# Retention of one decoder layer: score products within blocks of 128, preceding blocks through prefix sums of keys times values

## Chip, cores and metric

One core of a Trainium2 chip runs the kernel in one launch. The metric is device time in microseconds (us): the median over runs of the same program. TensorE is called PE here, VectorE DVE, ScalarE ACT, GpSimd POOL, and SyncE SP (it only issues transfers).

## The reference, cut to what matters

One layer for a prompt of 512 tokens and 8 sample tokens (D = 1024). The part that the change touches is the retention of the prompt, 4 heads of 128 columns, from a zero state:

```
q, k = rope(q), rope(k) * 128 ** -0.5
# for each head: gamma = 1 - 2 ** (-5 - head); for tokens r (query) and s (key)
o[r]  = sum over s <= r of gamma ** (r - s) * (q[r] . k[s]) * v[s]
s_new = sum over s of gamma ** (511 - s) * outer(k[s], v[s])       # an output
oc    = o - mean(o over its 128 columns)                            # then RMS norm, gain, silu gate
```

The reference itself walks over chunks of 128 tokens with a carried state; the sums are the same. Behind the mixer come the output projection, a router, 32 experts (top 2 of 8 in the best of 4 groups) and a gated per-layer embedding.

## The kernel before

PE works through a list of jobs written out in `job_list` (L52 to L75). Job number n writes the pair of PSUM banks n mod 4, so PE starts a job only when the engines that read job n - 4 are done with it (`Plan.free`, L138; READERS, L81, names the readers: A is ACT, D is DVE). All engines walk the same list in the same order: PE from L1613, ACT from L784, DVE from L1204. Each job ends with an increment of `pe_jobs`, and each reader counts up `act_jobs` or `dve_jobs`. The jobs around the change:

- **Chunks** ("q", "k", "v", "g", "gc", "hc", "gb", "wo"): a projection of 128 columns for all 520 tokens, 48 matmuls at L1563. Weights are split in two halves of fewer bits for each chunk: ACT makes the high half (L758), DVE the low half (`low_half`, L1147), both two chunks ahead. PE waits for both before a chunk.
- **q and k** are rotated after their chunk: ACT copies the swapped halves (L827, L828), then DVE runs three linked instructions (L1253 to L1255). PE needs the rotated rows for the scores.
- **scA, scB** (L1667): key block j (128 tokens) against queries of block j and all later ones, in widths 512, 384, 256 and 128, four matmuls for a head. DVE multiplies each by the decay while it reads PSUM (L1279 to L1284).
- **kt** (L1671): four transposes of the keys; DVE scales them (L1288), and then centres the values of the head over their 128 columns (`centre`, L1172: a reduction and a subtraction) into `v_mid`.
- **pv** (L1678): centred values times masked scores, again widths 512 to 128, accumulated in one bank, and copied by ACT (L838). With centred values the output needs no mean taken off later.
- **st** (L1684): four 128x128 products of scaled keys and values, accumulated into the state of the prompt; copied by ACT (L841), stored by POOL (L644).
- **gc, hc, gb**: the convolution. DVE's part of an hc job is long (L1309 to L1326).
- **state_row** (L1162): the state update of one of the 8 sample tokens, two DVE instructions 512 wide (L1167, L1169). VB_AT (L90) says after which chunks they run. All 8 must be done before PE starts "so" (L1654), the sample tokens' output. DVE centres that, "ot" transposes it (L1662), ACT squares the output of all four heads (L802), and "vs" (L1638) sums the squares. ACT takes the root, DVE the reciprocal (L1229), POOL stores it and loads it broadcast (L650, L653), and DVE waits for that in the first gate job, g0 (L1296).

In a head the order is scA, scB, kt, one chunk, pv, st, another chunk. After the projections (to about 260 us) come the router, an indirect load of the first expert's rows, and the experts, whose weights SP loads (2 MB a unit, three units an expert). The loads from unit 9 on wait for the experts' matmuls to free a slot (L551 to L568).

The original score and value products:

```
for half, j in enumerate((0, 1) if kind == "scA" else (2, 3)):
    width = SEQ - j * P
    last = mm(b[:, half * 512:half * 512 + width], kT[:, j * P:(j + 1) * P], qT[:, j * P:SEQ], ...)
```

Of the kernel before, what the change touches and what calls it, by code (L numbers as in the profile page):

```python
# [23 lines left out]
P = 128  # L24
# [9 lines left out]
H = 4  # L34
# [17 lines left out]
def job_list():  # L52

    jobs = [("v", 0), ("v", 1), ("v", 2), ("ss", 0), ("v", 3), ("rb", 0)]
    jobs += [("q", 0), ("vt", NT - 1), ("vt", 0), ("k", 0), ("vt", 1), ("vt", 2), ("q", 1), ("vt", 3)]

    def scores(h):
        return [("scA", h), ("scB", h), ("kt", h)]

    def sums(h):  # L60
        return [("pv", h), ("st", h)]
# [12 lines left out]
    jobs += [("rk", 0), ("ix", 0), ("iy", 0), ("tot", 0)]  # L74
    return jobs  # L75
# [4 lines left out]
LG_CUT = 256  # L80
READERS = dict(ss="A", rb="D", q="AD", k="AD", v="A", vt="A", g="D", so="D", ot="D", scA="D", scB="D", kt="D",  # L81
               pv="A", st="A", vs="A", lt="D", gc="D", hc="D", gb="D", wo="D", tp="A", lg="D",
               rk="D", ix="D", iy="D", tot="D", u="D", pa="A", pb="A", pg="A")
# [74 lines left out]
def build(nc, a, o):  # L158
# [9 lines left out]
    with ExitStack() as ctx:  # L168
# [86 lines left out]
        temp = ring[:, TEMP_SLOT, :]  # L255
        masked = [temp[:, i * 1280:(i + 1) * 1280] for i in range(2)]
        kd = [temp[:, 2560 + i * 512:3072 + i * 512] for i in range(2)]
        st_out = temp[:, 3584:4096].rearrange("p (h e) -> p h e", h=H)
        sq = [region_q[:, i * T:(i + 1) * T] for i in range(2)]
# [28 lines left out]
        o_few = sin_t[0:NB, 0:H * P]  # L288
        decay = region_d[:, :].rearrange("p (h r) -> p h r", h=H)
        gate_c = [region_z[:, i * T:(i + 1) * T] for i in range(2)]  # L290
# [86 lines left out]
        u_high, squared, sum_ready = sem("u_high"), sem("squared"), sem("sum_ready")  # L377
        silu_g, v_centred, o_squared, ret_made = sem("silu_g"), sem("v_centred"), sem("o_squared"), sem("ret_made")
        head_rstd, r_few_stored, r_wide_loaded = sem("head_rstd"), sem("r_few_stored"), sem("r_wide_loaded")
# [77 lines left out]
        def _(sp):  # L457
# [36 lines left out]
            for n in range(WIN_SLOTS, len(CHUNKS)):  # L494
# [6 lines left out]
                if n == 22:  # L501

                    sp.wait_ge(dve_jobs, HEAD.done("D", ("scB", H - 1)))
                    load_spare(0, 0)
                if n == 24:

                    sp.wait_ge(pe_jobs, HEAD.pe(("st", H - 1)))
                    sp.wait_ge(ret_stored, 16)
                    load_first(1)
# [107 lines left out]
        def _(pool):  # L617
# [24 lines left out]

            pool.wait_ge(act_jobs, HEAD.done("A", ("st", H - 1)))
            pool.dma_start(o["ret_p"], st_out).then_inc(ret_stored, 16)  # L644
# [93 lines left out]
        def _(act):  # L738
# [45 lines left out]
            for n, (kind, c) in enumerate(JOBS):  # L784
# [226 lines left out]
        def _(dve):  # L1011
# [192 lines left out]
            for n, (kind, c) in enumerate(JOBS):  # L1204
# [63 lines left out]
                elif kind == "ot":  # L1268
                    V.tensor_copy(qk[:, 0:H, SEQ:T], b[:, 0:H * NB].rearrange("p (h n) -> p h n", h=H)).then_inc(
                        dve_jobs, 1)  # L1270
                elif kind in ("scA", "scB"):

                    if (kind, c) == ("scA", 0):
# [3 lines left out]
                    dst = masked[c % 2]  # L1277
                    if kind == "scA":
                        link(V.tensor_tensor(dst[:, 0:512], b[:, 0:512], decay[:, c, 0:512], ALU.mult))  # L1279
                        V.tensor_tensor(dst[:, 512:896], b[:, 512:896], decay[:, c, 0:384],  # L1280
                                        ALU.mult).then_inc(dve_jobs, 1)
                    else:
                        link(V.tensor_tensor(dst[:, 896:1152], b[:, 0:256], decay[:, c, 0:256], ALU.mult))
                        V.tensor_tensor(dst[:, 1152:1280], b[:, 512:640], decay[:, c, 0:128],  # L1284
                                        ALU.mult).then_inc(dve_jobs, 1)
                elif kind == "kt":

                    V.tensor_tensor(kd[c % 2].rearrange("p (t d) -> p t d", t=4),  # L1288
                                    b[:, 0:512].rearrange("p (t d) -> p t d", t=4),
# [246 lines left out]
        def _(pe):  # L1536
# [76 lines left out]
            for n, (kind, c) in enumerate(JOBS):  # L1613
# [45 lines left out]
                elif kind == "ot":  # L1659
                    after("D", ("so", 0))  # L1660
                    for h in range(H):
                        last = tr(b[:, h * NB:(h + 1) * NB], o_few[:, h * P:(h + 1) * P], ident[0:NB, 0:NB])  # L1662
                elif kind in ("scA", "scB"):
                    kT, qT = qk[:, H + c, :], qk[:, c, :]
                    for half, j in enumerate((0, 1) if kind == "scA" else (2, 3)):
                        width = SEQ - j * P
                        last = mm(b[:, half * 512:half * 512 + width], kT[:, j * P:(j + 1) * P], qT[:, j * P:SEQ],  # L1667
                                  start=True, stop=True)
                elif kind == "kt":
                    for j in range(4):  # L1670
                        last = tr(b[:, j * P:(j + 1) * P], qk[:, H + c, j * P:(j + 1) * P], ident[:, :])  # L1671
                elif kind == "pv":
                    after("D", ("scB", c))
                    pe.wait_ge(v_centred, c + 1)
                    at = 0
                    for j in range(4):
                        width = SEQ - j * P
                        last = mm(b[:, j * P:SEQ], v_mid[:, j, c * P:(c + 1) * P], masked[c % 2][:, at:at + width],  # L1678
                                  start=(j == 0), stop=(j == 3))
                        at += width  # L1680
                elif kind == "st":
                    after("D", ("kt", c))
                    for j in range(4):
                        last = mm(b[:, 0:P], kd[c % 2][:, j * P:(j + 1) * P], v_rows[:, j, c * P:(c + 1) * P],  # L1684
                                  start=(j == 0), stop=(j == 3))
                elif kind == "tp":
# [208 lines left out]
def small_constants():  # L1895
# [8 lines left out]
    sin = np.sin(ang).astype(np.float32)  # L1904
    diff = np.arange(SEQ)[None, :] - np.arange(P)[:, None]
    decay = np.stack([np.where(diff >= 0, np.exp(np.float64(g) * np.maximum(diff, 0)), 0.0) for g in lg], 1) * SCALE
    left = (SEQ - 1 - np.arange(SEQ)).reshape(4, P).T
    kdec = np.stack([np.exp(np.float64(g) * left) for g in lg], 1) * SCALE
    token = np.zeros((P, NT), np.float32)
    for t, (r0, m) in enumerate(TILES):  # L1910
# [11 lines left out]
        cos=np.concatenate([cos, cos]), sin=np.concatenate([-sin, sin]),  # L1922
        decay=decay.reshape(P, H * SEQ).astype(np.float32), ident=np.eye(P, dtype=np.float32),
        meanw=np.full((P, P), 1.0 / P, np.float32),
# [78 lines left out]
```

## Time and profile before

| what | us |
|---|---|
| median of 3 runs | 830.74 (829.55 to 832.31) |
| profiled execution, its own time | 831.13 |
| its span in the trace | 829.3 |
| PE busy / DVE busy / ACT busy | 727.8 / 283.5 / 180.7 |

The trace is one execution; its time differs from the median by 0.39 us, and 1.8 us of it lie outside the span. Matmuls are pipelined in the records, so a single one's duration (272 ns and more) is longer than its share of a stream; the chain of waits gives the time from start to start. A float32 matmul shows as two records.

### The profile page before, as it was taken

To read this page: it belongs to the slowest core of one execution; us is meant where nothing else is said; L and a number is where in the kernel's file an instruction comes from. 1 tells how busy PE (TensorE), PEld (TensorE's weight loads), DVE (VectorE), ACT (ScalarE), POOL (GpSimd) and SP (SyncE) were. 2 spreads that over 40 slices of the span, in tenths; PEclk is the share of its full clock that TensorE was granted. 3 is DMA by queue.
4 is the path that set the end of the run, shared out by engine and by line. 5 is a ranking of instruction groups with operands and counts; after the bars stand their busy time and mean duration, and the time that the engine had idled before them with its cause. 6 is when DMAs were issued, how large, how long until landed. Compare 5 with 4: busy or idle time off the path is not lost.

```text
span 829.3 us, 11240 instructions
## 1 busy us (share of the span) xinstructions
PE 727.8 (88%) x4496; PEld 449.1 (54%) x4496; DVE 283.5 (34%) x504; ACT 180.7 (22%) x278; POOL 102.8 (12%) x161
## 2 busy tenths in 40 slices
PE   8999999999999789899999887777777777778996
PEld 8988899999998534333333322222222222226775
DVE  5556579766434521111101001001001001005875
ACT  7242321323322100111111110000000000004576
POOL 0500000000001112121121111111111111100000
PEclk9999999999999899999999999999999999999999
DMA  9641126572945799999999999999999999995301
GB/s 347 234 180 52 61 80 228 203 261 77 394 155 192 229 393 417 424 427 424 426 427 422 428 425 427 425 427 428 425 428 427 426 427 426 426 422 208 131 27 77
DMA packets 36457, 258.39 MB, mean 312 GB/s; under 512 B 7905, under 2 KB 8465, under 8 KB 22841
## 3 DMA queue, kind: packets, MB, share of 16 engines
q1 hardware_dynamic: 27248, 237.17, 70.0%
q0 software_dynamic: 7072, 19.07, 6.1%
q10 hardware_dynamic: 2096, 1.56, 0.6%
q8 instruction: 31, 0.51, 0.3%
q14 instruction: 10, 0.07, 0.0%
HBM read 251.04 MB, written 15.14 MB: 321 GB/s over the span
## 4 chain that ended last, share of the span: by engine, by line
PE 50%; DMA 35%; DVE 5%; ACT 2%; issue 2%; SPq 0%; DVEq 0%; POOLq 0%; ACTq 0%
DMA arena<-in_w_exp 33%; PE ps L1563 20%; PE ps L1759 15%; PE ps L1776 5%; PE ps L1890 2%; PE ps L1606 1%; PE ps L1678 1%; DMA region_u<-h_rows,index 1%; PE ps L1667 1%; DVE xh L1426 1%; DVE region_u L1379 1%; PE ps L1571 1%; DMA region_m<-y_rows 1%; PE ps L1767 1%; DMA y_rows<-region_v,both_cols 1%
## 5 line engine op out<-in xcount | busy, mean ns | idle before, releaser
L1759 PE MATMUL ps<-arena,region_u 128*64 128x512 f32 x960 | 218.9, 602 | 47.0 <-DMA arena<-in_w_exp 46.0
L1759 PEld LDWEIGHTS ps<-arena,region_u 128*64 128x64 f32 x960 | 67.0, 138 | 196.8 <-issue 124.7
L1375 DVE SCALAR_TENSOR_TENSOR region_u<-ps,small,region_u 128x256 f32<-128x256 f32 x32 | 15.5, 483 | 377.2 <-ACT region_u L864 377.2
L1563 PE MATMUL ps<-u_hi,w_hi 128*128 128x260 f32 x448 | 128.3, 286 | 4.5 <-issue 2.3
L1563 PE MATMUL ps<-u_lo,w_hi 128*128 128x260 f32 x448 | 126.6, 283 | 0.0
L1563 PE MATMUL ps<-u_hi,w_low 128*128 128x260 f32 x448 | 126.5, 282 | 0.0
L1776 PE MATMUL ps<-arena,region_u 128*64 128x512 f32 x480 | 109.6, 598 | 5.9 <-DVE region_u L1379 2.5
L1563 PEld LDWEIGHTS ps<-u_hi,w_hi 128*128 128x128 f32 x448 | 84.3, 188 | 6.2 <-issue 4.2
L1563 PEld LDWEIGHTS ps<-u_hi,w_low 128*128 128x128 f32 x448 | 84.5, 189 | 0.0
L1563 PEld LDWEIGHTS ps<-u_lo,w_hi 128*128 128x128 f32 x448 | 84.4, 188 | 0.0
L685 POOL DMA_INDIRECT y_rows<-region_v,both_cols x32 | 33.4, 1042 | 368.1 <-ACT region_v L868 368.1
L864 ACT ACTIVATE region_u<-ps,small 128x256 f32<-128x256 f32 x32 | 15.1, 473 | 267.3 <-PE ps L1759 267.3
L1776 PEld LDWEIGHTS ps<-arena,region_u 128*64 128x64 f32 x480 | 33.2, 136 | 63.0 <-issue 54.4
L868 ACT ACTIVATE region_v<-ps 128x512 f32<-128x512 f32 x32 | 19.1, 597 | 158.7 <-PE ps L1776 158.7
L1147 DVE TENSOR_TENSOR w_low<-arena,w_hi 128x1024 fp32r<-128x1024 f32 x35 | 42.6, 1220 | 20.2 <-ACT w_hi L758 20.0
L758 ACT ACTIVATE w_hi<-arena 128x1024 fp32r<-128x1024 f32 x35 | 36.7, 1049 | 25.0 <-PE ps L1563 24.9
L1563 PE MATMUL ps<-mix_lo,w_hi 128*128 128x260 f32 x128 | 36.2, 283 | 0.0
L1767 PE MATMUL ps<-ident,region_u 128*128 128x128 f32 x64 | 13.5, 293 | 25.4 <-DVE region_u L1375 25.3
L679 POOL DMA_INDIRECT region_u<-h_rows,both_cols x30 | 31.3, 1043 | 25.7 <-POOL both_cols L700 25.7
L1767 PEld LDWEIGHTS ps<-ident,region_u 128*128 128x128 f32 x64 | 7.1, 140 | 50.3 <-DVE region_u L1375 48.0
L1890 PE MATMUL ps<-gate_hi,u_hi 128*128 128x512 f32 (+1 forms) x72 | 26.8, 373 | 1.3 <-DVE u_lo L1449 1.3
L1890 PE MATMUL ps<-gate_lo,u_hi 128*128 128x512 f32 (+1 forms) x72 | 26.5, 367 | 0.0
(284 smaller groups left out, 855.8 us busy)
## 6 DMA issues: line engine op xcount, KB each, us to landing
arena<-in_w_exp SPq DMA_DIRECT2D x88, 2048.0 KB, 26.9
arena<-in_w_in SPq DMA_DIRECT2D x35, 512.0 KB, 4.3
region_q<-in_w_exp SPq DMA_DIRECT2D x24, 256.0 KB, 10.3
arena<-in_w_exp SPq DMA_DIRECT2D x8, 512.0 KB, 4.1
arena<-in_w_ple_gate SPq DMA_DIRECT2D x2, 2048.0 KB, 23.5
region_u<-in_xt SPq DMA_DIRECT2D x2, 1040.0 KB, 6.1
arena<-in_state_ret POOLq DMA_DIRECT2D x2, 1024.0 KB, 8.9
xh<-v_few POOLq DMA_DIRECT2D x1, 2048.0 KB, 9.1
```

The source lines that it names most:

```text
L679: pool.indirect_dma_start(out=xg[b], out_offset=None, in_=h_rows, in_offset=bass.IndirectOffsetOnAxis(ap=at, axis=0), bounds_check=2 * T - ...
L685: pool.indirect_dma_start(out=y_half, out_offset=bass.IndirectOffsetOnAxis(ap=scol[:, b:b + 1], axis=0), in_=out_sb[b], in_offset=None, bo ...
L758: nc.scalar.activation(w_hi[n % WIN_HIGH], w_raw[:, n % WIN_SLOTS, :], ACT.Copy).then_inc(w_hi_ready, 1)
L864: nc.scalar.activation(sg[b], ps[:, 2 + b, 0:256], ACT.Silu, scale=rs[b]).then_inc(out_sem, 1)
L868: nc.scalar.activation(out_sb[b], ps[:, 6 + b, :], ACT.Copy).then_inc(out_sem, 1)
L1147: V.tensor_tensor(w_low[:, n % WIN_SLOTS, :], w_raw[:, n % WIN_SLOTS, :], w_hi[n % WIN_HIGH], ALU.subtract).then_inc(w_lo_ready, 1)
L1375: V.scalar_tensor_tensor(hs[b], ps[:, 2 + b, 256:512], rs[b], sg[b], ALU.mult, ALU.mult).then_inc(out_sem, 1)
L1563: last = mm(halves(out)[:, half, :], w[:, k, :], u[:, cols], start=(k == 0 and s == 0), stop=(k == KD - 1 and s == 2))
L1759: last = mm(ps[side * 64:side * 64 + 64, 2 + b, :], xv[:, k // 4, k % 4, :], rows(k % 4 * 2 + side), start=(k == 0), stop=(k == KD - 1))
L1767: last = tr(ps[:, 4 + b, k * P:(k + 1) * P], hs[b][:, k * P:(k + 1) * P], ident[:, :])
L1776: last = mm(ps[side * 64:side * 64 + 64, 6 + b, :], hv, rows(q * 2 + side), start=(q == 0), stop=(q == 3))
L1890: last = mm(b[:, cols], u[:, k, :], w, start=(k == 0 and i == 0), stop=(k == KD - 1 and i == 2))
```

## The change

The scores are taken within a block only: four matmuls of width 128 for a head in one job, "sc". What earlier blocks give comes through the products that "st" already makes: they are no longer accumulated on PE but left as four separate sums. DVE forms the prefix sums, the last of which is the state output, then centres the three that are needed (`s_mid`), and PE multiplies them with `q_far`, the queries of tokens 128 to 511 times gamma ** (r - 511). The decay table keeps its size and holds both factors. `masked` and `kd` have one buffer instead of two. The order of jobs is new: in a head sc, kt, chunk, st, chunk, pv. gb0 moves up into the fourth head. Seven of the state updates run later by a chunk or two, and so, ot and vs stand after gc2, hc2 and gb2 instead of after hc1, gb1 and gc2.

```diff
-    jobs += scores(0) + [("k", 1)] + sums(0) + [("q", 2)] + scores(1) + [("k", 2)] + sums(1) + [("q", 3)]
-    jobs += scores(2) + [("k", 3)] + sums(2) + [("gc", 0)] + scores(3) + [("hc", 0)] + sums(3)
-    conv = [(kind, c) for c in range(CC) for kind in ("gc", "hc", "gb")]
-    between = [("so", 0), ("ot", 0), ("vs", 0)]
-    for n, job in enumerate(conv[2:]):
-        jobs += [job] + (between[n - 2:n - 1] if n >= 2 else [])
+    head = [("k", 1), ("q", 2), ("k", 2), ("q", 3), ("k", 3), ("gc", 0), ("hc", 0), ("gb", 0)]
+    for h in range(H):
+        jobs += [("sc", h), ("kt", h), head[2 * h], ("st", h), head[2 * h + 1], ("pv", h)]
+    between = {("gc", 2): ("so", 0), ("hc", 2): ("ot", 0), ("gb", 2): ("vs", 0)}
+    for job in [(kind, c) for c in range(1, CC) for kind in ("gc", "hc", "gb")]:
+        jobs += [job] + ([between[job]] if job in between else [])
...
-VB_AT = {("gc", 0): (0, 1), ("hc", 0): (2,), ("gb", 0): (3, 4, 5), ("gc", 1): (6, 7)}
+VB_AT = {("gc", 0): (0,), ("gb", 0): (1, 2, 3), ("gc", 1): (4, 5), ("gb", 1): (6, 7)}
...
-                elif kind == "st":
-
-                    nc.scalar.activation(st_out[:, c, :], b[:, 0:P], ACT.Copy).then_inc(act_jobs, 1)
...
-                    if kind == "scA":
-                        link(V.tensor_tensor(dst[:, 0:512], b[:, 0:512], decay[:, c, 0:512], ALU.mult))
-                        V.tensor_tensor(dst[:, 512:896], b[:, 512:896], decay[:, c, 0:384],
-                                        ALU.mult).then_inc(dve_jobs, 1)
-                    else:
-                        link(V.tensor_tensor(dst[:, 896:1152], b[:, 0:256], decay[:, c, 0:256], ALU.mult))
-                        V.tensor_tensor(dst[:, 1152:1280], b[:, 512:640], decay[:, c, 0:128],
-                                        ALU.mult).then_inc(dve_jobs, 1)
+                    link(V.tensor_tensor(q_far, qk[:, c, P:SEQ], far[:, c, :], ALU.mult))
+                    V.tensor_tensor(masked.rearrange("p (j r) -> p j r", j=4), b[:, 0:SEQ].rearrange("p (j r) -> p j r", j=4),
+                                    decay[:, c, :].unsqueeze(1).to_broadcast([P, 4, P]), ALU.mult).then_inc(dve_jobs, 1)
+                elif kind == "st":
+
+                    sums = b[:, 0:SEQ].rearrange("p (j e) -> p j e", j=4)
+                    link(V.tensor_copy(s_mid[:, 0, :], sums[:, 0, :]))
+                    for j in (1, 2):
+                        link(V.tensor_tensor(s_mid[:, j, :], s_mid[:, j - 1, :], sums[:, j, :], ALU.add))
+                    V.tensor_tensor(st_out[:, c, :], s_mid[:, 2, :], sums[:, 3, :], ALU.add).then_inc(dve_jobs, 1)
+                    dve.wait_ge(dve_jobs, done)
+                    centre(s_mid, s_mid, col["vm"][:, 0:3], [P, 3, P]).then_inc(s_centred, 1)
...
-                elif kind in ("scA", "scB"):
-                    kT, qT = qk[:, H + c, :], qk[:, c, :]
-                    for half, j in enumerate((0, 1) if kind == "scA" else (2, 3)):
-                        width = SEQ - j * P
-                        last = mm(b[:, half * 512:half * 512 + width], kT[:, j * P:(j + 1) * P], qT[:, j * P:SEQ],
-                                  start=True, stop=True)
+                elif kind == "sc":
+                    for j in range(4):
+                        at = slice(j * P, (j + 1) * P)
+                        last = mm(b[:, at], qk[:, H + c, at], qk[:, c, at], start=True, stop=True)
...
-                    at = 0
+                    pe.wait_ge(s_centred, c + 1)
                     for j in range(4):
-                        width = SEQ - j * P
-                        last = mm(b[:, j * P:SEQ], v_mid[:, j, c * P:(c + 1) * P], masked[c % 2][:, at:at + width],
-                                  start=(j == 0), stop=(j == 3))
-                        at += width
+                        at = slice(j * P, (j + 1) * P)
+                        last = mm(b[:, at], v_mid[:, j, c * P:(c + 1) * P], masked[:, at], start=True, stop=(j == 0))
+                        if j:
+                            last = mm(b[:, at], s_mid[:, j - 1, :], q_far[:, (j - 1) * P:j * P], start=False, stop=True)
...
                     for j in range(4):
-                        last = mm(b[:, 0:P], kd[c % 2][:, j * P:(j + 1) * P], v_rows[:, j, c * P:(c + 1) * P],
-                                  start=(j == 0), stop=(j == 3))
+                        at = slice(j * P, (j + 1) * P)
+                        last = mm(b[:, at], kd[:, at], v_rows[:, j, c * P:(c + 1) * P], start=True, stop=True)
```

## Rows read from the trace of the kernel before

**Rows 1.** The page's chain that ended last: shares of the span by engine.

```profile
PE 50%; DMA 35%; DVE 5%; ACT 2%; issue 2%; SPq 0%; DVEq 0%; POOLq 0%; ACTq 0%
```

**Rows 2.** Stretches: length, busy time of PE, PEld, DVE, ACT, POOL, PEclk, DMA share, GB/s.

```profile
218.00:262.00 44.00, 43.72 (x392) 41.69 (x391) 14.86 (x22) 12.43 (x24) 3.88 (x6) 1.00 0.53 186
285.00:296.00 11.00, 9.79 (x36) 3.15 (x37) 4.22 (x16) 0.47 (x1) 1.40 (x3) 0.79 0.92 318
310.00:436.00 126.00, 120.91 (x582) 44.71 (x578) 17.40 (x44) 13.22 (x24) 25.18 (x40) 1.00 1.01 425
436.00:748.00 312.00, 243.24 (x1112) 81.62 (x1108) 33.19 (x80) 25.02 (x48) 46.91 (x76) 1.00 1.01 426
```

**Rows 3.** Chain that ended last, one head of retention: start us, us, what.

```profile
58.36 0.63 PE ps L1671 x4
58.99 5.77 PE ps L1563 x48
...
66.91 0.89 PE ps L1684 x8
67.81 5.73 PE ps L1563 x48
73.54 2.16 PE ps L1667 x8
75.69 0.44 PE ps L1671 x4
...
77.27 5.99 PE ps L1563 x48
83.26 2.16 PE ps L1678 x8
```

**Rows 4.** DVE's instructions in order of time, 60 to 77 us.

```profile
60.64 0.29 DVE L1284 TENSOR_TENSOR arena<-ps,region_d 128x128 f32<-128x128 f32 x1
61.04 0.69 DVE L1288 TENSOR_TENSOR arena<-ps,small 128x512 f32<-128x512 f32 x1
62.96 1.22 DVE L1147 TENSOR_TENSOR w_low<-arena,w_hi 128x1024 fp32r<-128x1024 f32 x1
...
75.00 0.70 DVE L1253 TENSOR_TENSOR region_q<-ps,trig 128x520 f32<-128x520 f32 x1 [4.67 <-ACT region_z L828]
...
76.47 0.70 DVE L1255 TENSOR_TENSOR region_q<-region_q,region_z 128x520 f32<-128x520 f32 x1
```

**Rows 5.** Chain that ended last, behind the heads and at the experts' start.

```profile
121.94 17.20 PE ps L1563 x144
...
146.94 0.34 PE ps L1662 x4
147.28 5.94 PE ps L1563 x48
...
275.84 7.03 DMA region_u<-h_rows,index
...
285.03 9.41 PE ps L1759 x32
...
300.20 6.89 PE ps L1759 x32
```

**Rows 6.** DVE in order of time: an hc job, first and last; the reciprocal.

```profile
139.21 0.06 DVE L1309 MEMSET region_z<- 128x2 f32 x1 [0.66 <-PE ps L1563]
...
143.40 0.69 DVE L1326 TENSOR_TENSOR region_m<-arena 128x512 f32<-128x512 f32 x1
...
155.04 3.40 DVE L1229 RECIPROCAL region_q<-region_q 128x520 f32<-128x520 f32 x1 [0.85 <-ACT region_q L843]
```

**Rows 7.** ACT in order of time: the squares between ot and vs.

```profile
149.17 2.20 ACT L802 ACTIVATE region_q<-region_q 128x520 f32<-128x520 f32 x4
```

**Rows 8.** DMA issues: the broadcast that g0 waits for, KB, us to landing.

```profile
region_q<-r_few POOLq DMA_DIRECT2D x1, 1040.0 KB, 7.7
```

**Rows 9.** PE's waits by line and releaser: us in total, times, longest.

```profile
PE ps L1759 <- DMA arena<-in_w_exp: 46.0, 39, 1.4
```

**Rows 10.** Weight loads of the 128-wide products st: min, median, max ns.

```profile
L1684 PEld LDWEIGHTS ps<-region_v,arena x32: 192/192/192, 66.6 to 121.6; 128*128 128x128 f32 x32
```

More of the change, by code:

```diff
@@ L80 @@
 LG_CUT = 256
-READERS = dict(ss="A", rb="D", q="AD", k="AD", v="A", vt="A", g="D", so="D", ot="D", scA="D", scB="D", kt="D",
-               pv="A", st="A", vs="A", lt="D", gc="D", hc="D", gb="D", wo="D", tp="A", lg="D",
+READERS = dict(ss="A", rb="D", q="AD", k="AD", v="A", vt="A", g="D", so="D", ot="D", sc="D", kt="D",
+               pv="A", st="D", vs="A", lt="D", gc="D", hc="D", gb="D", wo="D", tp="A", lg="D",
                rk="D", ix="D", iy="D", tot="D", u="D", pa="A", pb="A", pg="A")
@@ L255, in build @@
         temp = ring[:, TEMP_SLOT, :]
-        masked = [temp[:, i * 1280:(i + 1) * 1280] for i in range(2)]
-        kd = [temp[:, 2560 + i * 512:3072 + i * 512] for i in range(2)]
-        st_out = temp[:, 3584:4096].rearrange("p (h e) -> p h e", h=H)
+        masked, kd = temp[:, 0:SEQ], temp[:, SEQ:2 * SEQ]
+        st_out = temp[:, 2 * SEQ:3 * SEQ].rearrange("p (h e) -> p h e", h=H)
+        q_far = temp[:, 3 * SEQ:4 * SEQ - P]
+        s_mid = temp[:, 4 * SEQ - P:5 * SEQ - 2 * P].rearrange("p (j e) -> p j e", j=3)
         sq = [region_q[:, i * T:(i + 1) * T] for i in range(2)]
@@ L288, in build @@
         o_few = sin_t[0:NB, 0:H * P]
-        decay = region_d[:, :].rearrange("p (h r) -> p h r", h=H)
+        decay = region_d[:, 0:H * P].rearrange("p (h r) -> p h r", h=H)
+        far = region_d[:, H * P:H * SEQ].rearrange("p (h r) -> p h r", h=H)
         gate_c = [region_z[:, i * T:(i + 1) * T] for i in range(2)]
@@ L377, in build @@
         u_high, squared, sum_ready = sem("u_high"), sem("squared"), sem("sum_ready")
-        silu_g, v_centred, o_squared, ret_made = sem("silu_g"), sem("v_centred"), sem("o_squared"), sem("ret_made")
+        silu_g, v_centred, s_centred, o_squared, ret_made = (
+            sem("silu_g"), sem("v_centred"), sem("s_centred"), sem("o_squared"), sem("ret_made"))
         head_rstd, r_few_stored, r_wide_loaded = sem("head_rstd"), sem("r_few_stored"), sem("r_wide_loaded")
@@ L501, in _ @@
                 if n == 22:
-                    sp.wait_ge(dve_jobs, HEAD.done("D", ("scB", H - 1)))
+                    sp.wait_ge(dve_jobs, HEAD.done("D", ("sc", H - 1)))
                     load_spare(0, 0)
                 if n == 24:
-                    sp.wait_ge(pe_jobs, HEAD.pe(("st", H - 1)))
+                    sp.wait_ge(pe_jobs, HEAD.pe(("pv", H - 1)))
                     sp.wait_ge(ret_stored, 16)
@@ L641, in _ @@
             pool.dma_start(o["conv_s0"], a["state_conv"][:, 1, :]).then_inc(misc_stored, 16)
-            pool.wait_ge(act_jobs, HEAD.done("A", ("st", H - 1)))
+            pool.wait_ge(dve_jobs, HEAD.done("D", ("st", H - 1)))
             pool.dma_start(o["ret_p"], st_out).then_inc(ret_stored, 16)
@@ L1662, in _ @@
                         last = tr(b[:, h * NB:(h + 1) * NB], o_few[:, h * P:(h + 1) * P], ident[0:NB, 0:NB])
[L1663 to L1668 removed]
+                elif kind == "sc":
+                    for j in range(4):
+                        at = slice(j * P, (j + 1) * P)
+                        last = mm(b[:, at], qk[:, H + c, at], qk[:, c, at], start=True, stop=True)
                 elif kind == "kt":
@@ L1672, in _ @@
                 elif kind == "pv":
-                    after("D", ("scB", c))
+                    after("D", ("sc", c))
                     pe.wait_ge(v_centred, c + 1)
-                    at = 0
+                    pe.wait_ge(s_centred, c + 1)
                     for j in range(4):
-                        width = SEQ - j * P
-                        last = mm(b[:, j * P:SEQ], v_mid[:, j, c * P:(c + 1) * P], masked[c % 2][:, at:at + width],
-                                  start=(j == 0), stop=(j == 3))
-                        at += width
+                        at = slice(j * P, (j + 1) * P)
+                        last = mm(b[:, at], v_mid[:, j, c * P:(c + 1) * P], masked[:, at], start=True, stop=(j == 0))
+                        if j:
+                            last = mm(b[:, at], s_mid[:, j - 1, :], q_far[:, (j - 1) * P:j * P], start=False, stop=True)
                 elif kind == "st":
@@ L1904, in small_constants @@
     sin = np.sin(ang).astype(np.float32)
-    diff = np.arange(SEQ)[None, :] - np.arange(P)[:, None]
+    diff = np.arange(P)[None, :] - np.arange(P)[:, None]
     decay = np.stack([np.where(diff >= 0, np.exp(np.float64(g) * np.maximum(diff, 0)), 0.0) for g in lg], 1) * SCALE
+    far = np.stack([np.tile(np.exp(np.float64(g) * (np.arange(P, SEQ) - SEQ + 1)), (P, 1)) for g in lg], 1)
+    decay = np.concatenate([decay.reshape(P, H * P), far.reshape(P, H * (SEQ - P))], 1)
     left = (SEQ - 1 - np.arange(SEQ)).reshape(4, P).T
@@ L1922, in small_constants @@
         cos=np.concatenate([cos, cos]), sin=np.concatenate([-sin, sin]),
-        decay=decay.reshape(P, H * SEQ).astype(np.float32), ident=np.eye(P, dtype=np.float32),
+        decay=decay.astype(np.float32), ident=np.eye(P, dtype=np.float32),
         meanw=np.full((P, P), 1.0 / P, np.float32),
```

9 lines of the change are left out of this document (2 added, 7 removed).

## The prediction, made before the changed kernel ran

> **What bounds the kernel now.** I read the shares of the chain first: half of the span is PE, a third is DMA [rows 1]. The stretches tell where. Up to the output projection PE is busy all the time, with its clock at the full 2.4 GHz level [rows 2]. From about 290 us on the DMA engines are full: share 1.01 from 310 to 748 us, at 425 GB/s, while PE has slack behind 436 us. So the experts are bound by the weight stream. Its length is fixed by its bytes, and its start by PE: the loads of unit 9 and later wait until the first expert's matmuls free a slot. Between 218 and 262 us the DMA share is 0.53, so no old traffic holds that start back. So whatever the retention stage saves on PE moves the first expert, the stream and the end by as much. The stages behind are unchanged, and the change is worth what it is worth in PE's chain between 54 and 154 us.
>
> In that chain [rows 3] PE is the bound but for one thing: the next key chunk starts only when the query chunk before it is rotated. The query chunk ends at 73.54, DVE's last rotation instruction ends at 76.47 + 0.70 = 77.17 [rows 4], and the key chunk starts at 77.27, 3.73 us behind the query chunk's end. PE fills 2.60 of these with scores and transposes and idles 1.14. The chunk behind the idle time then takes 5.99 us instead of 5.74.
>
> **PE's work.** Scores: 1280 columns for a head take 2.16 us (L1667, eight records), or 0.108 us for 128 columns of a record. What is new is 128 columns wide throughout, and the nearest row of such products is st: eight records in 0.89 us, 0.111 each. I take 0.111. Scores: 8 x 0.111 = 0.89, so 1.27 less for each head. pv: four products within blocks and three with the prefix sums, 14 records, 1.55 us instead of 2.16, 0.60 less. st has the same products (their start flags cost nothing: the count of columns is the same) and kt is untouched. Over four heads that is 7.5 us less work; how much of it reaches the end depends on what PE waits for.
>
> **Start to start on PE.**
> - Head 0. kt0 waits today for the rotation of q1 and starts at 58.36; k1 follows at 58.99. In the new order kt0 reuses an older bank pair and runs earlier, but k1 waits for the same rotation, so it starts at 58.36: 0.63 gained. It then carries the 0.22 that follow an idle spell (5.99 against 5.77). Gain 0.41. PE's idle time there grows to about 2.0 us.
> - From the end of k1 to the start of k2. Today: pv 2.16 + st 0.89 + q2 5.73 + 3.73 = 12.51. New: st 0.89 + q2 5.73 + 3.73 = 10.35. pv (1.55), sc (0.89) and kt (0.44) are 2.88 and lie within the 3.73, which the rotation sets; 0.85 stay idle. Gain 2.16: here the order hides the whole of pv. From k2 to k3 the same. Together 4.3.
> - From the end of k3 to the end of pv3: pv2, scores 3 and pv3 are shorter by 0.60 + 1.27 + 0.60 = 2.47.
>
> Sum 7.2 us, if no new wait comes.
>
> **DVE's work, and the waits that it adds.** Per head DVE loses the multiplications of widths 512, 384, 256 and 128 and gains q_far (384) and one of 512, about 0.75 less. It gains the sums: a copy and three additions 128 wide, 0.29 each with 0.03 between them [rows 4], then a reduction and a subtraction 384 wide. For 384 I take 0.56, between 0.29 for 128 and 0.69 for 512. With 0.1 where it waits for its own result or for PE: 1.3 + 1.2 + 0.2 = 2.7 us. The bounds are 2.2 (every instruction at 0.29) and 4.5 (every one at 0.69). ACT loses its copy of st, 4 times, which nobody waits for.
>
> PE needs the centred sums at pv. With K the end of a key chunk: rotation ends at K + 3.63, the sums at K + 6.3; PE has done st and the chunk behind it at K + 0.89 + 5.74 = K + 6.63. So pv0, pv1 and pv2 have 0.3 us to spare. Behind the sums DVE has the low half of a chunk (1.22) before the next rotation, which ACT's copies let start 1.46 behind the query chunk; that leaves 0.57.
>
> pv3 is different: between hc0 and st3 DVE works off hc0, from 0.07 behind PE's end to 4.26 later at the last instruction's start and 0.69 more [rows 6], so 4.95. The sums are there at 4.95 + 2.7 = 7.65 behind hc0's end, while PE has st3 and gb0 done at 0.89 + 5.74 = 6.63. **PE waits 1.0 us at pv3.** Behind that wait on PE stands gc1, and everything after it.
>
> State updates: each is two instructions 512 wide, 1.4. The second to fourth run behind gb0, the next two behind gc1, the last two behind gb1. With F the end of gb0, and the low halves (1.22), evacuations (0.70) and hc1 in between, I get the eighth done at F + 23.9, while PE, with pv3 behind it and four chunks, gets to so at F + 25.7. Cost nothing; without these 1.8 us of cover, so waits.
>
> **so, ot and vs one group later.** Here I see the second new wait. Today ot stands behind gb, on which DVE has just 0.70 us of work, so the squares are early. In the new list ot stands behind hc2, and DVE finishes the whole convolution first. With T the end of hc2: ot's copy is done at T + 5.3, ACT's four squares take 2.20 [rows 7], so T + 7.6, and PE can start vs at T + 7.7. PE has ot (0.34) and gb2 (5.94) behind it at T + 6.28 [rows 5]. **PE waits 1.4 us at vs.** The way to g0 gets shorter too: PE is at the end of g0 by about T + 32, four chunks behind vs. The squares, ACT's high half (about 1.0, as DVE's 1.22), DVE's low half and evacuation of gb2, ACT's copy of it, the root and the reciprocal of 3.40 end near T + 15.5; the broadcast lands in 7.7 [rows 8], and if the store before it took as long, the end would be T + 31. It is hidden, also past POOL's other transfers, which are done by then. SP's loads around it (units 0 and 1, behind chunk loads) wait for the same jobs and have tens of us before the experts.
>
> Each new wait also makes PE's next work some 0.2 longer (0.63 against 0.44 for kt, 5.99 against 5.74 for a chunk): 0.4 for both.
>
> **Sum.** 7.2 - 1.0 - 1.4 - 0.4 = 4.4, taken as 4.3 for the extra semaphore wait at each pv. Against the profiled execution 831.13 - 4.3 = 826.8; against the median, which is 0.39 lower, 830.74 - 4.3 = **826.4 us**.
>
> **Rivals.**
> - *The two waits do not come* (DVE ahead of my walk): 830.7 - 7.2 = 823.6. For it: the sums' lower bound of 2.2 takes half off pv3's wait. Against: ot behind hc2 is plain order on DVE. Chance 0.12, still faster.
> - *The clock.* PE idles 7 us before the first expert, and the stretch behind it ran at a granted clock of 0.79; its 32 matmuls took 9.41 instead of 6.89 [rows 2, 5]. PE's idle spells of up to 1.4 us left the clock at 1.00 [rows 9, 2]. The new 2.0 us at k1 lies between. If it costs the same 2.5 us: 828.9, within the noise. Chance 0.06. It can hardly happen twice, as the other waits are no longer than those that held.
> - *128 columns do not pay.* If the weight load showed behind every narrow product, 192 ns each [rows 10], scores would take 1.54 and pv 2.69. Then pv, sc and kt are 4.67, no longer within 3.73; k1 to k3 gain 1.2 each, the rest loses 0.44, and with both waits the gain is about 0.0: 830.7. Against: the st row itself, 0.89 for eight, shows loads hidden. Chance 0.03. The Trainium skill, page "TensorE: Matmul & The Clock Gate", section "Back-to-back issue gap", gives about 81 ns for a sustained pair of load and matmul of 128 columns against about 131 ns for 512. By that, as an estimate, narrower scores would shrink by about a third only, pv with its 14 records would get longer, and the change would bring next to nothing on PE. This trace disagrees: its time goes by columns, 0.108 against 0.111.
> - *Hidden by the stream or given back later*: no change, 830.7. Against: the load's start follows PE. Chance 0.05.
> - *Slower: DVE's sums become the bound, at every pv.* If the chain took x us more than 2.7, pv3 costs x, pv2 x - 0.3, the rotations of q2 and q3 x - 0.57 each, so the gain is 5.7 - 4x. It is slower by over 0.3% from x = 2.1, a chain of 4.8; at 5.0 it gives 834.2. For it: six dependent short instructions right in front of what PE waits for. Against: even with all at 0.69 it is 4.5, 832. Chance 0.05.
>
> **How the numbers follow.** About 0.3%, 2.5 us, is what a measurement of this kernel can tell from no change. My forecast has 0.69 and is faster; with the first rival 0.81, of which I give 0.02 to same for a pv wait longer than I have it. Same: 0.06 + 0.03 + 0.05 + 0.02, less a little that goes to either side: 0.15. Slower 0.05. Low end: the first rival less the spread of runs, 822.8. High end: clock rival and sums of 3.2 us, 829.3.
>
> **What would show it right or wrong.** In the chain of the changed kernel: scores in 0.89 and pv in 1.55 for a head; about 10.35 from the end of k1 to the start of k2, set by the rotation; PE idle 2.0 before k1, 0.85 before k2 and k3, 1.0 before pv3 on the centred sums and 1.4 before vs on ACT's squares; the first expert's matmuls near 285.0 - 4.3 = 280.7; the clock at 1.00 from 54 to 154 us. The sum is wrong if the sums on DVE take over 3 us, if pv0 to pv2 wait, or if the stream does not start earlier with the first expert.

## The result and the profile after

The changed kernel takes 825.31 us (median of 6 runs, 821.47 to 827.34), the kernel before on the same occasion 830.32 (828.78 to 832.31). The ratio is 0.994 (95% interval 0.9921 to 0.9959): faster by 5.0 us, where 4.3 were forecast. On two later occasions the same kernel took 822.49 and 822.29 beside 829.35 and 829.71, so the gain lies between 5 and 7.5 us, by the occasion. The profiled execution took 825.39, with a span of 823.6.

The chain that ended last, for heads 0 and 1 (start us, us, what). Line numbers have moved: L1647 is vt3 (the last transposes of the values, the landmark from which stages are measured below), L1560 a chunk, L1663 the scores, L1666 kt, L1680 st, L1673 and L1675 the seven products of pv (two records each).

```profile
54.54 0.44 PE ps L1647 x4
54.98 0.91 PE ps L1663 x8
55.88 0.69 ACT region_v L832
56.57 1.69 issue
58.27 7.53 PE ps L1560 x48
65.79 0.89 PE ps L1680 x8
66.68 5.74 PE ps L1560 x48
...
74.32 0.89 PE ps L1663 x8
75.21 0.44 PE ps L1666 x4
75.65 0.51 issue
76.16 6.01 PE ps L1560 x48
82.17 0.89 PE ps L1680 x8
83.06 5.74 PE ps L1560 x48
88.80 0.44 PE ps L1673 x4
...
90.36 0.89 PE ps L1663 x8
91.25 0.44 PE ps L1666 x4
91.69 0.84 issue
92.53 5.98 PE ps L1560 x48
```

The scores take 0.89 us instead of 2.16, pv 1.56 (88.80 to 90.36) instead of 2.16. From the end of k1 (65.79) to the start of k2 (76.16) are 10.37 us, and 10.36 from k2 to k3; the kernel before has 12.51 [rows 3]. One thing is off: k1, behind the longer idle time, takes 7.53 us instead of the 5.77 of [rows 3].

The same profile in stretches (us; length; busy time of PE, PEld, DVE, ACT, POOL; PEclk, DMA share, GB/s): the clock fell to half (1.2 GHz) when k1 began behind the idle time, and came back before 62 us.

```profile
58.00:60.00 2.00, 1.74 (x8) 1.76 (x9) 1.84 (x4) 0.00 (x0) 0.00 (x0) 0.59 0.00 0
60.00:62.00 2.00, 2.00 (x12) 2.00 (x11) 1.86 (x4) 0.00 (x0) 0.00 (x0) 0.56 0.00 0
62.00:64.00 2.00, 2.00 (x19) 2.00 (x18) 1.28 (x2) 0.00 (x0) 0.00 (x0) 1.00 0.00 0
```

PE's waits between 40 and 260 us (us in total, times, longest): both new waits are there, at vs (L1635) and at pv3 (L1673), and the three idle times before key chunks.

```profile
PE ps L1560 <- issue: 3.3, 3, 2.0
PE ps L1635 <- ACT region_q L799: 1.3, 1, 1.3
PE ps L1673 <- DVE arena L1169: 1.0, 1, 1.0
```

DVE's sums in head 3, in order of time, from the end of hc0's work: 2.4 us from 118.76 to 121.20 for six instructions, and 0.14 later PE starts pv3 at 121.34.

```profile
118.03 0.69 DVE L1323 TENSOR_TENSOR region_m<-arena 128x512 f32<-128x512 f32 x1
118.76 0.29 DVE L1277 COPY arena<-ps 128x128 f32<-128x128 f32 x1
119.09 0.61 DVE L1279 TENSOR_TENSOR arena<-arena,ps 128x128 f32<-128x128 f32 x2
119.73 0.29 DVE L1280 TENSOR_TENSOR arena<-arena,ps 128x128 f32<-128x128 f32 x1
120.05 0.55 DVE L1168 TENSOR_REDUCE small<-arena 128x3 f32<-128x384 f32 x1
120.64 0.56 DVE L1169 SCALAR_TENSOR_TENSOR arena<-small,arena 128x384 f32<-128x384 f32 x1
```

And the way into the experts, from the chain again: the router's last matmuls (L1704), the indirect load, the first expert.

```profile
257.22 2.15 PE ps L1704 x20
...
272.76 5.11 DMA region_u<-h_rows,index
...
279.57 8.81 PE ps L1754 x32
290.48 3.65 PE ps L1771 x16
```

Where the 5.7 us between the two spans (829.3 and 823.6) come from, by three landmarks: the transposes vt3, the start of the router's last matmuls, the first expert's down projection. From vt3 to the router 205.88 became 202.84 (3.04 less). From there to the down projection 36.24 became 33.26 (2.98 less). The rest, from there to the end, 532.75, became 533.12 (and 0.05 lies ahead of vt3). So half of the gain seen here is in a stage that the change does not touch, and the stretch that it does touch gave less than the 4.3 of the forecast. Both had to be explained.

### The profile page after: what moved, and what is told of

The parts are those of the page before. It is cut to its first block, busy times and chain, and to the rows that moved or that the text cites. A ratio compares the mean times of both kernels' runs of the same rounds, so it can differ in the third digit from the quotient of the medians.

```text
span 823.6 us, 11299 instructions
## 1 busy us (share of the span) xinstructions
PE 721.8 (88%) x4520; PEld 450.1 (55%) x4520; DVE 288.8 (35%) x520; ACT 179.6 (22%) x274; POOL 102.6 (12%) x161
## 3 DMA queue, kind: packets, MB, share of 16 engines
q10 hardware_dynamic: 2096, 1.56, 0.6%
## 4 chain that ended last, share of the span: by engine, by line
PE 53%; DMA 36%; DVE 6%; ACT 3%; issue 2%; SPq 0%; DVEq 0%; POOLq 0%; ACTq 0%
DMA arena<-in_w_exp 33%; PE ps L1560 23%; PE ps L1754 15%; PE ps L1771 5%; PE ps L1885 3%; PE ps L1603 1%; DMA region_q<-in_xt 1%; DVE xh L1423 1%; DVE region_u L1376 1%; DMA region_u<-h_rows,index 1%; DMA region_m<-y_rows 1%; PE ps L1568 1%; DMA y_rows<-region_v,both_cols 1%; PE ps L1762 1%; PE ps L1673 0%
## 5 line engine op out<-in xcount | busy, mean ns | idle before, releaser
L1372 DVE SCALAR_TENSOR_TENSOR region_u<-ps,small,region_u 128x256 f32<-128x256 f32 x32 | 15.5, 484 | 376.7 <-ACT region_u L858 376.7
L1560 PE MATMUL ps<-u_hi,w_hi 128*128 128x260 f32 x448 | 129.2, 288 | 5.1 <-issue 3.3
L1560 PE MATMUL ps<-u_lo,w_hi 128*128 128x260 f32 x448 | 127.4, 284 | 0.0
L1560 PE MATMUL ps<-u_hi,w_low 128*128 128x260 f32 x448 | 127.3, 284 | 0.0
L1560 PEld LDWEIGHTS ps<-u_hi,w_hi 128*128 128x128 f32 x448 | 85.1, 190 | 7.0 <-issue 5.0
L1560 PEld LDWEIGHTS ps<-u_hi,w_low 128*128 128x128 f32 x448 | 85.2, 190 | 0.0
L1560 PEld LDWEIGHTS ps<-u_lo,w_hi 128*128 128x128 f32 x448 | 85.2, 190 | 0.0
L1560 PE MATMUL ps<-mix_lo,w_hi 128*128 128x260 f32 x128 | 36.2, 283 | 0.0
```

Source lines behind the costliest of these rows:

```text
L1372: V.scalar_tensor_tensor(hs[b], ps[:, 2 + b, 256:512], rs[b], sg[b], ALU.mult, ALU.mult).then_inc(out_sem, 1)
L1560: last = mm(halves(out)[:, half, :], w[:, k, :], u[:, cols], start=(k == 0 and s == 0), stop=(k == KD - 1 and s == 2))
```

## The experiments

The landmarks of all profiles but that of e8_products_only stand here first, since several readings need them together. "Retention": from vt3 to the router's last matmuls. "k1": that chunk. "Stores": from the router's last matmuls to SP's next load, which waits until the rows stored for the experts have landed. "Load": the first indirect load. "First 32": the first expert's first matmuls. "Router": from the router's last matmuls to the first down projection. All in us. What lies ahead of vt3 is left out: it took 54.0 to 56.1 us, without a pattern by kernel, so totals and start times of single profiles are off by up to 2 us for that alone.

| profile | retention | k1 | stores | load | first 32 | router |
|---|---|---|---|---|---|---|
| before | 205.88 | 5.77 | 13.02 | 7.03 | 9.41 | 36.24 |
| e5_before | 205.89 | 5.74 | 13.05 | 6.55 | 9.73 | 35.83 |
| e6_before2 | 205.87 | 5.74 | 13.05 | 5.63 | 8.81 | 35.28 |
| e7_order_only | 204.34 | 5.75 | 12.87 | 6.69 | 9.51 | 35.96 |
| e11_before_more_code | 205.88 | 5.74 | 12.48 | 4.71 | 8.81 | 34.27 |
| changed | 202.84 | 7.53 | 11.85 | 5.11 | 8.81 | 33.26 |
| e1_same | 201.27 | 5.99 | 11.78 | 4.00 | 7.11 | 31.94 |
| e12_same_again | 201.27 | 5.98 | 11.70 | 4.04 | 7.11 | 32.00 |
| e2_fill | 200.81 | 5.96 | 11.97 | 5.19 | 8.81 | 34.84 |
| e3_pv_later | 199.80 | 6.00 | 11.83 | 7.51 | 8.75 | 36.05 |
| e4_vs_later | 201.46 | 7.52 | 12.06 | 4.21 | 7.11 | 32.15 |
| e9_both_later | 200.13 | 7.50 | 11.83 | 7.25 | 9.28 | 36.34 |
| e10_all_three | 198.61 | 5.99 | 11.74 | 5.05 | 8.68 | 34.50 |

**The changed kernel again (e1_same, e12_same_again), no edit.**

> The changed kernel again, nothing edited. Its first profile has a gain of 4.5 us up to the convolution, 3.1 us up to the router and 5.5 us at the first expert's matmuls, because the first indirect load took 5.11 us instead of 7.03. Theory 1: that load's time changes from execution to execution (it shares the DMA engines with weight loads), so here it lies anywhere from 5 to 7 us, and the 3.1 us are the change's own gain. Rival: the change shortens it (its weight loads start at another moment); then it is near 5.1 us again. Both expect the chunk k1 at 7.5 us with a granted clock near 0.56 for its first part, and PE's waits of 2.0, 1.0 and 1.3 us before k1, pv3 and vs. Time near 825.3.

> The changed kernel once more, for its own scatter beside the two above: 822 to 826. Clock at k1: dips (7.5 us) or does not (6.0). From vt3 to the router 201.3, or 202.8 with the dip; the stores' landing 5.5 to 5.8 us behind POOL's instruction.

Measured: 822.49 us, ratio 0.9919 (0.9903 to 0.9936), and 822.29, ratio 0.9909 (0.989 to 0.9928). k1 took 5.99 and 5.98 us although PE idled 2.0 before it, and the retention stretch 201.27 both times. The chain of e1_same:

```profile
57.33 1.69 issue
59.03 5.99 PE ps L1560 x48
65.02 0.89 PE ps L1680 x8
```

So the change's own gain in its stretch is 205.88 - 201.27 = 4.6 us, and of the three profiles of this kernel the clock took 1.57 of them in the first only. That k1 would be slow each time was wrong: it is a dip that comes in some executions. The indirect load scatters (4.00, 4.04, 5.11), as the first theory had it, though under its 5 to 7. The stores of e12_same_again landed 5.2 us behind POOL's instruction, a little under the range.

**The idle time before k1 filled (e2_fill).**

```diff
                 last.then_inc(pe_jobs, 1)
+                if (kind, c) == ("kt", 0):
+                    spin(b[:, 512:640], 7)
```

> Seven 128-wide matmuls into the unused second bank of kt0's pair, behind its increment, fill about 1.55 of the 2.0 us that PE idles before k1. Theory: the idle time let the granted clock fall, and k1 takes 7.53 us for it; with the gap filled the clock stays at 1.00, k1 takes 5.8 to 6.0, the start of k1 does not move, and everything behind is 1.5 to 1.7 us earlier: about 823.7. Rival: k1 is slow because of what DVE and ACT read and write beside it; then k1 stays at 7.5 and the time at 825.3.

Measured: 825.08 us, ratio 0.9938 (0.9924 to 0.9953). The clock stays at 1.00 and k1 takes 5.96; but with the dip absent from e1_same as well, one profile shows nothing. Over all profiles: behind 2.0 us of idle time k1 dipped in three of seven (changed, e4_vs_later, e9_both_later; not in e1_same, e12_same_again, e3_pv_later and e8_products_only); filled, in none of two (here and e10_all_three); behind 1.2 us, as before, in none of five. That is in line with the theory, and too few to prove it. The median lies 2.6 us over e1_same's, with overlapping intervals. In the two profiled executions the difference is in the router stage (34.84 against 31.94) and ahead of vt3 (1.0), not in retention (200.81 against 201.27); for the median no more is shown.

**pv3 behind the chunk gc1 (e3_pv_later).**

```diff
+    jobs[-1:] = [("gc", 1), jobs[-1]]
...
-    for job in [(kind, c) for c in range(1, CC) for kind in ("gc", "hc", "gb")]:
+    for job in [(kind, c) for c in range(1, CC) for kind in ("gc", "hc", "gb")][1:]:
```

> pv3 moved behind the chunk gc1. Theory: the 1.0 us before pv3 is a wait for the centred sums alone, with PE's next 0.2 us slower behind it; behind gc1 the sums are 4.7 us old, so PE has no wait there and what follows is 1.0 to 1.2 us earlier: about 824.2. Rival: DVE is the bound in this stretch (state updates, convolution), and the time comes back as a wait at so or at a chunk; then the time is within 0.3 us of e1_same at the start of vs.

Measured: 821.8 us, ratio 0.9904 (0.9889 to 0.9918). Retention takes 199.80, 1.47 less than 201.27, and of PE's waits in the stretch only these two are left, beside one of 0.3 just before the router that every profile has:

```profile
PE ps L1561 <- issue: 3.3, 3, 2.0
PE ps L1636 <- ACT region_q L800: 1.3, 1, 1.3
```

The wait at pv3 was for the sums alone, and nothing takes its place. At the start of so the gain is 1.22, the wait and the slower matmuls behind it, as expected. The other 0.25 comes behind vs, where nine chunks take 51.8 us instead of 52.1; why is open. The total, 0.7 us under e1_same's, does not tell the two apart: the intervals overlap.

**ot behind gb2, vs behind gc3 (e4_vs_later).**

```diff
-    between = {("gc", 2): ("so", 0), ("hc", 2): ("ot", 0), ("gb", 2): ("vs", 0)}
+    between = {("gc", 2): ("so", 0), ("gb", 2): ("ot", 0), ("gc", 3): ("vs", 0)}
```

> ot moved behind gb2 and vs behind gc3. Theory: the 1.3 us before vs is DVE working off hc2 before it copies ot, then ACT's squares of 2.2 us; one chunk later they are done, PE has no wait, and the projections end 1.3 to 1.5 us earlier: about 823.9. Rival: the broadcast for g0, now some 4 us later, becomes late: DVE waits for it at g0 for about 1 us, and if PE waits behind that, part or all of the 1.3 us is lost again at the gate chunks or at wo.

Measured: 822.32 us, ratio 0.9909 (0.9896 to 0.9922). PE's waits have no line for vs:

```profile
PE ps L1560 <- issue: 3.3, 3, 2.0
...
PE ps L1673 <- DVE arena L1169: 1.0, 1, 1.0
```

Retention takes 201.46 with k1 at 7.52. Without that dip of 1.53 it would be 199.93, 1.34 less than 201.27. The broadcast is still hidden. The total is level with e1_same's (822.49), so this gain, too, is seen in the stretch alone.

**The kernel before again (e5_before, e6_before2), no edit.**

> The kernel before, looked at again for a second profile. From the router's last matmuls (L1709, start) to the first expert's down projection (L1776, start) its first profile took 36.2 us, with an indirect load of 7.03; five profiles of changed kernels took 31.9 to 36.1, with loads of 4.0 to 7.5 and, in three of them, a clock below 1.00 before the router ends. Theory 1: that stage scatters in every kernel, so here it lies in the same range and may well be under 35. Rival: it is long in the kernel before always, and the change shortens it, by which the gain is 4.3 to 4.8 us of retention and some 2 us of this stage; then it is near 36 again.

> The kernel before, a third profile. The same two expectations as for the second. In the retention stage both theories expect the same as the first profile: 205.9 us from the transposes of the values (vt3) to the router's last matmuls, and a clock of 1.00 between 54 and 154 us.

Measured: 830.41 and 829.99 us. Retention 205.89 and 205.87, within 0.02 of the first profile: that stretch has almost no scatter, so single profiles can be compared there. The router stage takes 35.83 and 35.28. Neither theory holds as it was put. It scatters (by 1 us here, by 4.4 over the changed kernels), but with the old products it is also long: 35.3 to 36.2 in four profiles (34.27 in e11_before_more_code, which is edited for this stage), against 31.9 to 36.3, mean 33.9, in eight with the narrow ones. The column "stores" is split cleanly: 12.9 to 13.05 against 11.7 to 12.06.

**The new order alone (e7_order_only).** The kernel before, with the new list of jobs and state updates (and SP's wait for the last retention job adapted to it), and all products as they were.

```diff
-    jobs += scores(0) + [("k", 1)] + sums(0) + [("q", 2)] + scores(1) + [("k", 2)] + sums(1) + [("q", 3)]
...
+    for h in range(H):
+        jobs += [("scA", h), ("scB", h), ("kt", h), head[2 * h], ("st", h), head[2 * h + 1], ("pv", h)]
```

> The kernel before with the new order of jobs and of state updates alone: scores of all widths, pv of all widths, st accumulated on PE. Theory: pv moves into the time of the rotation. Between key chunks PE has st 0.89, a chunk 5.73, pv 2.16, scores 2.16 and kt 0.44, 11.38 us instead of 12.51, twice; no wait at pv3, since there are no centred sums; the wait before vs stays (1.3 us, and 0.2 behind it). Sum 0.7 us less than before in the stretch up to the router. Rival: the order is worth nothing or the narrower products carry it all (4 us and more without it); then the stretch is 205.9 or longer and the gain of the change lies in the products alone.

Measured: 828.52 us beside 829.28, ratio 0.9989 (0.9976 to 1.0003). Retention 204.34, 1.54 less than before. The chain of its head 1, where nothing idles before the key chunk at 93.02:

```profile
75.90 5.74 PE ps L1563 x48
81.64 0.89 PE ps L1684 x8
82.54 5.73 PE ps L1563 x48
88.26 2.16 PE ps L1678 x8
90.42 2.16 PE ps L1667 x8
92.58 0.44 PE ps L1671 x4
93.02 5.74 PE ps L1563 x48
```

11.38 us from k2 to k3, as expected. Of the 0.8 us that were missed, 0.5 are the slower matmuls behind two idle times, which are gone too: 5.74 instead of the 5.99 of [rows 3]. The rest is the wait before vs, which costs about 1.3 with what follows, not 1.5. So the order gives 1.5 of the 4.6 us in the stretch; the total gained 0.8 us, with an interval that includes no change.

**The narrow products in the old order of pv (e8_products_only).**

```diff
-        jobs += [("sc", h), ("kt", h), head[2 * h], ("st", h), head[2 * h + 1], ("pv", h)]
+        jobs += [("sc", h), ("kt", h), head[2 * h], ("st", h), ("pv", h), head[2 * h + 1]]
```

> The changed kernel with pv straight behind st, as in the order before; all else as changed. Theory: pv waits for the rotation and for DVE's sums, 5.4 us behind st in heads 0 to 2 and 6.7 us in head 3, which the chunk between them hides in the changed kernel. The key chunks no longer wait for the query's rotation, so heads 0 and 1 lose 4.7 each, head 2 loses 5.4 and head 3 loses 5.7: 20 us longer than the changed kernel, about 845, more if the clock falls in waits of 5 us. Rival: DVE is done early enough that the order matters by under 5 us.

Measured: 854.55 us in its one run, where 845 were expected; retention 232.7 (287.02 - 54.28), 31.5 over e1_same. PE's waits:

```profile
PE ps L1673 <- DVE arena L1169: 23.6, 4, 6.7
```

and stretches of it, columns as above:

```profile
60.00:75.00 15.00, 9.17 (x62) 9.01 (x61) 7.47 (x13) 1.96 (x4) 0.00 (x0) 0.83 0.11 37
90.00:105.00 15.00, 10.39 (x64) 10.43 (x65) 5.34 (x10) 1.54 (x2) 0.00 (x0) 0.77 0.07 26
```

The four waits are of the expected size (5.4 to 6.7 us; they end at 70.87, 94.61, 118.59 and 143.59). The rest over the expected 20 us goes with the clock, which fell behind each of the four: in stretches of 5 us it was 0.50 from 70 us on, 0.50 from 95, 0.54 from 120 and 0.65 from 145, and back at 1.00 in between. PE's busy time there times the missing share of the clock comes to some 11 us (an estimate from these stretches), which is the difference. So the narrow products pay only because a chunk stands between st and pv. To add it up as 1.5 for the order and 3.1 for the products would be wrong: the products without their place for pv make the stretch 27 us longer than before.

**More code in the kernel before (e11_before_more_code).** SPIN_FIRST (L95) is 26 instead of 14.

> The kernel before with 12 more filling matmuls at its start (26 instead of 14), 48 more PE records like the changed kernel has. In four profiles with the old products the last rows stored for the router land 6.8 to 7.0 us after POOL's last store instruction, in five with the narrow ones 5.5 to 5.8. In the former an instruction fetch of PE (q8, 5.8% of 16 engines in one us, so 0.93 us of one engine) and another (q14, 0.3 us) run 6 and 7 us behind the router's last matmuls, among the stores; in the latter they do not. Theory: where in the code a fetch falls decides 0.9 to 1.2 us there, so here, with the fetch some 5 us earlier, the stores land 5.7 to 6.1 us after the instruction, and the first expert starts about 1 us earlier counted from the router's matmuls. Rival: it is what the change leaves in memory or in the queues; then it stays at 6.8 to 7.0.

Why this was tried: in the kernel before, one microsecond from 266 us on, the DMA queues (packets, MB, share of 16 engines) are

```profile
q1 hardware_dynamic: 30, 0.49, 114.9%
q8 instruction: 1, 0.02, 5.8%
```

This is one packet of code, 5.8% of 16 engines, so 0.93 us on a single one, while the last rows are being stored; what follows the stores waits until the last of them has landed. With the narrow products the packet comes 11 to 16 us behind the router's last matmuls, when the stores are nearly or fully done. Measured: retention 205.88 as before; in the 14 us from 1 us ahead of the router's last matmuls on no q8 packet is left, and q14's is; "stores" 12.48 instead of 13.04. From POOL's instruction it is 5.5 us, under the expected 5.7 to 6.1, but that number flatters, since the instruction itself came 0.9 us later behind a dip of the clock. The gain of "about 1 us" was half that. So 0.56 of the 1.2 us between the two groups went with the place of a piece of code, in one profile, against a scatter of 0.03 in three of the kernel before (e7_order_only, also with the old products, has 12.87). That q8 carries PE's code is shown by the same edit, which moved its packet and left q14's. That q14's packet is the rest was not tried.

**Both waits removed, and the gap filled (e9_both_later, e10_all_three).** The edits of e3_pv_later and e4_vs_later together, then with e2_fill's.

> The changed kernel with pv3 behind gc1, ot behind gb2 and vs behind gc3. Theory: both waits go, as they did one at a time, and nothing takes their place. Projections from vt3 to the router's last matmuls: 201.3 in the changed kernel without the clock's dip at k1, less 1.2 and 1.4, so 198.7 (or 200.2 with the dip). Time 2 us and more under the changed kernel, about 820 to 821. Rival: the two edits share one slack of DVE, and together they give no more than one alone (199.8).

> The same, and the seven filling matmuls before k1. Theory: the dip of the clock at k1 (7.5 instead of 6.0 us, in two of four executions with an idle time of 2.0) does not come, so the stretch is 198.2 to 198.7 in every execution, and the median is up to 1 us under e9_both_later. Rival: what the filling adds in PE instructions costs as much elsewhere, as e2_fill's median, above e1_same's, might say; then it is level or slower.

Measured: e9_both_later 822.85 us (818.04 to 826.23), ratio 0.9895 (0.9871 to 0.992); e10_all_three 820.98 (819.52 to 821.97), ratio 0.9886 (0.9866 to 0.9905). Retention 200.13 with k1 at 7.50, which is 198.62 without its dip of 1.51, and 198.61: both edits together give 2.7 us, where they gave 1.47 and 1.34 one at a time. The rival of one shared slack is out. In the total e10_all_three has the lowest median, 1.3 us under e12_same_again on the same occasion, with overlapping intervals. For e9_both_later the expected total of 820 to 821 was missed: it is level with e12_same_again. Its profile, the slowest of its six executions, shows why the total says little: the router stage took 36.34 us, with a load of 7.25 and

```profile
281.00 9.28 PE ps L1755 x32
```

## Why the prediction was right

The forecast of 4.3 us stands against 4.6 measured in its stretch without the dip, and 5.0 to 7.4 in the total. In the stretch each step holds. In e1_same the gain is 0.45 up to the end of k1 (forecast 0.41), 4.31 from there to the end of k3 (4.3), 1.27 from there to the end of pv3 (2.47 less 1.2 for the wait and what follows it), and 1.42 are lost behind it, where the wait at vs lies (1.6); gb0, which changed places, is counted as before. In the total it was in part luck that the first occasion came so near: in its profile the dip took 1.6 us and the router stage gave 3.0.

- **PE's work.** 0.89 for the scores and 1.56 for pv, against 0.89 and 1.55. Time goes by columns at this width here. The rule of the Trainium skill that I weighed (page "TensorE: Matmul & The Clock Gate", section "Back-to-back issue gap") would have made pv longer; here seven products of 128 columns take less than the four wide ones did.
- **The order.** 10.37 and 10.36 us between key chunks, against 10.35. pv lies within the rotation; e8_products_only shows what it would cost elsewhere.
- **pv3 and vs.** 1.0 and 1.3 us of wait, against 1.0 and 1.4, and taking them away gave 1.47 and 1.34, against 1.2 and 1.6 with what follows. The sums took 2.4 us with 0.14 to PE's start, against 2.7 with both gaps.
- **The clock.** The rival had it that 2.0 us of idle time might lower the clock, at 2.5 us and a chance of 0.06. It happens, in three of seven profiles, and costs 1.5 us (7.50 to 7.53 against 5.98 to 6.00): the chance was far too low and the price too high, because I took it from the first expert, behind 7 us of idle time [rows 5]. I treated it as all or nothing for the kernel, when it is drawn anew in every execution. The Trainium skill, same page, section "What's actually happening", says that the windows in which the activity is looked at run free of the kernel's start. Whether a gap counts could then differ from execution to execution, and so it does here, where the same program has k1 at 7.53, 5.99 and 5.98; no run here shows the windows themselves.
- **Sum.** The term missing is the router stage. I wrote that the stages behind are unchanged, and the change worth what it is worth on PE before them. For the code this holds; for the time it does not. The stage is on average 1.9 us shorter (33.9 against 35.8), of which 1.2 lie in the stores' landing, and 0.56 of these go with a fetch of code. The first expert's matmuls started at 279.57 in the first profile, where 280.7 was forecast. The rest is in the indirect load and the clock at the first expert: loads of 4.0 to 4.2 us left the first 32 matmuls at 7.11, loads of 4.7 and more had them at 8.7 to 9.7. Part of the load's length is its start. In seven of the 13 profiles of the table (e6_before2, e11_before_more_code, e1_same, e12_same_again, e2_fill, e4_vs_later, e10_all_three) the clock fell to half for some 3 us in the router's own work, PE was late with the matmuls that fill its waiting time, and the load started 17.0 us behind the router's last matmuls and took 4.0 to 5.6 us. In the other six the clock stayed at 1.00 there, the load started at 15.5 and took 5.1 to 7.5. That draw fell on five of the eight narrow kernels and on one of the four old ones, so the part of the 1.9 us beyond the stores is not shown to be an effect of the change. What else moves the load's end is open. It shares the DMA engines with weight loads that SP issues when the stores have landed, and in 9 of the 13 profiles of the table it ends 8.8 to 9.6 us behind these, but not in all.

## What to carry to other kernels

Before narrower products are counted as a gain, look at who makes the operand that they need, and put a full piece of other work between that engine's start and the product: here the same arithmetic was worth 5 us or cost 25, by the place of one job. Compare two profiles by landmarks inside the kernel, and take a second profile of each kernel before a stage that the change does not touch is called part of its effect: retention agreed to 0.02 us between executions of the same kernel but for the dip of the clock, the router stage differed by 1.0 and 1.3. An idle time of PE that is harmless in one profile can cost the clock in the next.

## What was not expected of the hardware

Half clock behind an idle time of 2.0 us on PE, in three of seven executions of otherwise equal work, for 1.5 us of loss each; none behind 1.2 us in five. The same fall, to half, behind each of four idle times of 5.4 to 6.7 us in e8_products_only. A single packet of PE's instruction code held a DMA engine for 0.93 us (5.8% of 16 engines in one microsecond). Moving it away from the stores, by 12 unrelated matmuls at the start of the program, made SP's next load, which waits for the stores, 0.56 us earlier in one profile.
